# A gated convolution and its output projection become one stage, the projection's rows of two chunks first; the MLPs' down products wait for the half of the hidden rows that each panel uses

## The reference, cut to what matters

```python
def mixer_b(h, w_in, conv_w, w_out):
    b_gate, c_gate, xt = jnp.split(h @ w_in, 3, axis=-1)
    u = c_gate * xt
    y = lax.conv_general_dilated(u, ...)          # depthwise, three taps along the tokens
    return (b_gate * y) @ w_out

def mlp_sq_relu(h, w1, w2):
    return jnp.square(jax.nn.relu(h @ w1)) @ w2   # 1024 -> 4096 -> 1024

for i in range(DEPTH_2):
    y = rms_norm_2(h, norm1[i])
    y = mixer_a(...) or mixer_b(...)              # layer 0: attention, layer 1: mixer_b
    h = h + y
    h = h + mlp_sq_relu(rms_norm_2(h, norm2[i]), mlp_w1[i], mlp_w2[i])
```

## Time and profile before

| what | before |
|---|---|
| median of three runs | 3050.26 us |
| the profiled execution's own time | 3053.55 us |
| its span | 3051.8 us |
| PE busy | 2784.8 us, 91% |
| DVE, ACT, POOL busy | 37%, 30%, 26% |

### The profile page before, as it was taken

How to read it: one execution, slowest core, us unless ns; L and a number is a source line. 1 busy time by engine, 2 the same in 40 slices (tenths; PEclk the granted TensorE clock), 3 DMA queues, 4 the chain that set the end, 5 groups by cost and what they waited for, 6 DMA issues and landing times. The chain is left out here.

```text
span 3051.8 us, 56007 instructions
## 1 busy us (share of the span) xinstructions
PE 2784.8 (91%) x25293; PEld 2147.4 (70%) x25293; DVE 1119.5 (37%) x1536; ACT 921.8 (30%) x1462; POOL 789.0 (26%) x222
## 2 busy tenths in 40 slices
PE   6987988888896988989999999988999999899998
PEld 4765877777774423333689989987888778678887
DVE  3424765666346000101454556363211123321111
ACT  3123322432432100010444555553322222132222
POOL 3220431231210000000232332321444434334443
PEclk8998999999997999999999999999999999999999
DMA  7111201013041999999322221321223323223321
GB/s 260 56 32 39 70 17 61 4 60 102 4 133 42 420 427 426 427 427 426 135 79 73 80 70 56 84 83 56 91 97 98 99 72 97 83 83 97 97 97 56
DMA packets 171635, 397.69 MB, mean 130 GB/s; under 512 B 9552, under 2 KB 99637, under 8 KB 146037
## 3 DMA queue, kind: packets, MB, share of 16 engines
q1 hardware_dynamic: 170416, 390.70, 34.9%
q10 hardware_dynamic: 980, 3.40, 0.3%
HBM read 387.71 MB, written 4.19 MB: 128 GB/s over the span
## 5 line engine op out<-in xcount | busy, mean ns | idle before, releaser
L179 POOL TENSOR_TENSOR weight_ring_lo<-weight_ring,weight_hi 128x2048 fp32r<-128x2048 f32 (+1 forms) x144 | 656.5, 4559 | 1928.0 <-ACT weight_hi L168 1887.6
L168 ACT CAST weight_hi<-weight_ring 128x2048 fp32r<-128x2048 f32 (+1 forms) x144 | 271.2, 1885 | 640.3 <-PE late L226 339.7
L226 PE MATMUL late<-weight_hi,latT_hi 128*128 128x512 f32 x572 | 175.3, 429 | 0.0
L207 PE MATMUL late<-latT_hi,weight_hi 128*128 128x512 f32 x680 | 167.9, 389 | 0.0
L207 PE MATMUL late<-latT_lo,weight_hi 128*128 128x512 f32 x680 | 167.9, 389 | 0.0
L207 PE MATMUL late<-latT_hi,weight_ring_lo 128*128 128x512 f32 x680 | 167.9, 389 | 0.0
L1924 POOL TENSOR_TENSOR rws_E<-rws_AT,rw_tri 128x768 f32<-128x768 f32 x40 | 83.5, 2112 | 284.4 <-DVE rws_AT L1808 183.7
L226 PE MATMUL late<-weight_ring_lo,latT_hi 128*128 128x512 f32 x572 | 156.5, 396 | 0.0
L226 PE MATMUL late<-weight_hi,latT_lo 128*128 128x512 f32 x572 | 155.8, 394 | 0.0
L226 PE MATMUL late<-weight_hi,mlp_hid_hi 128*128 128x512 f32 x512 | 138.7, 393 | 9.8 <-issue 9.8
L3278 DVE TENSOR_TENSOR x<-x,late 128x512 f32<-128x512 f32 x64 | 44.0, 687 | 280.8 <-PE late L226 280.8
(11 more groups left out here) (630 smaller groups left out, 5339.5 us busy)
## 6 DMA issues: line engine op xcount, KB each, us to landing
weight_ring<-in_mlp_w SPq DMA_DIRECT2D x64, 1024.0 KB, 5.2
weight_ring<-in_a_wqkv SPq DMA_DIRECT2D x36, 1024.0 KB, 4.8
weight_ring<-in_w_up SPq DMA_DIRECT2D x32, 1024.0 KB, 20.2
weight_ring<-in_w_gate SPq DMA_DIRECT2D x31, 1024.0 KB, 22.2
weight_ring<-in_w_down SPq DMA_DIRECT2D x31, 1024.0 KB, 21.0
weight_ring<-in_w_mod SPq DMA_DIRECT2D x24, 1024.0 KB, 5.5
weight_hi_spare<-in_w_up SPq DMA_DIRECT2D x12, 1024.0 KB, 19.9
weight_hi_spare<-in_w_gate SPq DMA_DIRECT2D x12, 1024.0 KB, 22.2
```

The costliest lines, as they stand in the source:

```text
L168: self.nc.scalar.copy(self.view(self.hi[:, q % 2], p, True), self.view(self.slots[self.slot[p]], p, True)).then_inc(self.hi_ready, 1)
L179: self.nc.gpsimd.tensor_tensor(self.view(self.lo[:, s], p, True), self.view(self.slots[s], p, True), self.view(self.hi[:, q % 2], p, True) ...
L207: last = nc.tensor.matmul(dst, left(a, k), right(b, k), start=(a + b + k == 0), stop=(a == 1 and k == KD - 1))
L226: last = nc.tensor.matmul(dst, left(a, HK * r + k), right(b, k), start=(r + a + b + k == 0), stop=(r == 1 and a == 1 and k == HK - 1))
```

## The change

`gated_conv` takes over the projection: the four panels of `b_wout` are multiplied in the same block, behind the last chunk's panels, and its calls to the norm come with it. The panels are now ordered rows first, as those of `w_out` already are: first rows 0 to 511 (the first two chunks of z) for both halves of the columns, then rows 512 to 1023. PE waits for the copies of b and c (banks 0 to 3 are free), for two z chunks before the first two panels (`lowered`), for all four before the last two, and within the second panel it does the tiles of banks 6 and 7 first and waits for `emptied` ahead of banks 4 and 5. In `mlp` the one wait ahead of a quarter's down panels becomes two: the first down panel waits for two hidden chunks, the second for four.

```diff
@@ -3202,8 +3202,8 @@
                         else:
                             last = dense(nc, up[i % 2][h][:], left, right)
                 else:
-                    if n == 0:
-                        pe.wait_ge(hidden, NP * (q + 1))
+                    if n < 2:
+                        pe.wait_ge(hidden, NP * q + NP // 2 * (n + 1))
                     for j in range(NT):
                         u = NT * (2 * q + n // 2) + j
                         if n % 2 == 0 and u >= NT:
@@ -3289,7 +3289,7 @@
     return norm
 
 
-def gated_conv(nc, g, yT, z_hi, z_lo, banks, ahead):
+def gated_conv(nc, g, yT, z_hi, z_lo, banks, ahead, x, norm_of):
 
     sem, st = g.sem, g.stream
     p0 = st.taken
@@ -3297,17 +3297,22 @@
     copied = sem("gc_b_c_copied")
     rounded = sem("gc_rounded")
     step = Tally(sem("gc_steps"))
-    n_chunk = D // PW
+    lowered = sem("gc_lowered")
+    filled = sem("b_wout_filled")
+    added = sem("b_wout_first_half_added")
+    n_chunk, n_panel = D // PW, 2 * D // WIDE
+    p1 = p0 + 3 * n_chunk
     with ExitStack() as tmp, nc.Block() as block:
         bc = tmp.enter_context(nc.sbuf_tensor("gc_bc", [P, 2, 2, 2, T], F32))
         u = tmp.enter_context(nc.sbuf_tensor("gc_u", [P, 2, T], F32))
         y = tmp.enter_context(nc.sbuf_tensor("gc_y", [P, 2, T], F32))
         z = tmp.enter_context(nc.sbuf_tensor("gc_z", [P, 2, 2, T], F32))
         acc = [banks[2 * s:2 * s + 2] for s in range(3)]
+        norm = norm_of(tmp, [b[:] for b in banks])
 
         @block.sync
         def _(sp):
-            st.load_until(sp, p0 + 3 * n_chunk)
+            st.load_until(sp, p1 + n_panel)
 
         @block.tensor
         def _(pe):
@@ -3326,10 +3331,27 @@
                     else:
                         last = dense(nc, acc[part][h][:], left, right)
                 last.then_inc(st.used, 1)
+            for n in range(n_panel):
+                w = st.take_split(pe)
+                c, r = n % 2, n // 2
+                if n == 0:
+                    pe.wait_ge(copied, 2 * n_chunk)
+                if c == 0:
+                    pe.wait_ge(lowered, n_chunk // 2 * (r + 1))
+                for j in (2, 3, 0, 1) if n == 1 else range(NT):
+                    if n == 1 and j == 0:
+                        pe.wait_ge(emptied, n_chunk)
+                    last = dense_half(nc, banks[NT * c + j][:], lambda a, k: (z_hi, z_lo)[a][:, k, j * P:(j + 1) * P],
+                                      lambda b, k: w[b][:, k, :], r)
+                    if r and j + 1 < NT:
+                        last.then_inc(filled, 1)
+                last.then_inc(st.used, 1)
+            pe.wait_ge(added, 1)
+            norm.turn(pe)
 
         @block.gpsimd
         def _(pool):
-            st.reduce_until(pool, p0 + 3 * n_chunk + 2)
+            st.reduce_until(pool, p1 + n_panel + 1)
 
         @block.scalar
         def _(act):
@@ -3353,6 +3375,14 @@
                     split(c - 1)
                 st.round_until(act, p0 + 3 * c + 5)
             split(n_chunk - 1)
+            st.round_until(act, p1 + n_panel + 1)
+            for j in range(NT):
+                norm.square(act, j)
+                if j:
+                    norm.root(act, j - 1)
+            norm.root(act, NT - 1)
+            for k in range(LEAD):
+                norm.round(act, k)
 
         @block.vector
         def _(dve):
@@ -3363,7 +3393,7 @@
 
             def lower(c):
                 dve.wait_ge(rounded, c + 1)
-                V.tensor_tensor(z_lo[:, 2 * c:2 * c + 2], z[:, c % 2], z_hi[:, 2 * c:2 * c + 2].bitcast(F32), ALU.subtract)
+                V.tensor_tensor(z_lo[:, 2 * c:2 * c + 2], z[:, c % 2], z_hi[:, 2 * c:2 * c + 2].bitcast(F32), ALU.subtract).then_inc(lowered, 1)
 
             for c in range(n_chunk):
                 if c:
@@ -3389,6 +3419,24 @@
                 last.then_inc(emptied, 1)
                 dve.wait_ge(emptied, c + 1)
             lower(n_chunk - 1)
+            for c in range(2):
+                for j in range(NT):
+                    if j + 1 < NT:
+                        dve.wait_ge(filled, (NT - 1) * c + j + 1)
+                    else:
+                        dve.wait_ge(st.used, p1 + 3 + c)
+                    d = x[:, j, c * WIDE:(c + 1) * WIDE]
+                    last = V.tensor_tensor(d, d, banks[NT * c + j][:], ALU.add)
+                    if c:
+                        last.then_inc(norm.x_ready, 1)
+                        if j:
+                            norm.scale(dve, j - 1)
+                if c == 0:
+                    last.then_inc(added, 1)
+            norm.scale(dve, NT - 1)
+            for k in range(LEAD):
+                norm.lower(dve, k)
+    return norm
 
 
 def program(nc, a, out):
@@ -3450,9 +3498,12 @@
             st.add((w[:, r0 + hp * P:r0 + (hp + 1) * P], 0), (w[:, r0 + 512 + hp * P:r0 + 512 + (hp + 1) * P], P), n_slot=3)
         st.add_matrix(a["w_mod"], 0, 2 * D, 6 * D - D // 2, split=False, n_slot=2)
         st.add_matrix(a["w_mod"], 0, 6 * D - D // 2, 6 * D, split=False)
-        for r in range(0, D, D // 2):
-            for c in range(0, D, WIDE):
-                st.add((a["w_out"][r:r + D // 2, c:c + WIDE], 0), row=WIDE)
+        def add_rows_first(w):
+            for r in range(0, D, D // 2):
+                for c in range(0, D, WIDE):
+                    st.add((w[r:r + D // 2, c:c + WIDE], 0), row=WIDE)
+
+        add_rows_first(a["w_out"])
         st.add_slots([None] * 4, [lasting(f"slot{s}_full") for s in range(SLOTS, SLOTS + 4)])
 
         def add_gate_up(e):
@@ -3488,7 +3539,7 @@
         for c in range(0, D, PW):
             for part in range(3):
                 st.add((a["b_win"][:, part * D + c:part * D + c + PW], 0))
-        st.add_wide(a["b_wout"], 0, 0, D)
+        add_rows_first(a["b_wout"])
         add_mlp(1)
 
         with ExitStack() as first:
@@ -3683,8 +3734,7 @@
             with ExitStack() as tmp:
                 z_hi = g.sb_in(tmp, "gc_z_hi", [P, KD, T], F32R)
                 z_lo = g.sb_in(tmp, "gc_z_lo", [P, KD, T], F32R)
-                gated_conv(nc, g, yT, z_hi, z_lo, banks, ahead)
-                ahead = project_rows(nc, g, "b_wout", lambda i, k: (z_hi, z_lo)[i][:, k], x, normed("norm2_1", "norm2", 1, True), banks)
+                ahead = gated_conv(nc, g, yT, z_hi, z_lo, banks, ahead, x, normed("norm2_1", "norm2", 1, True))
             mlp(nc, g, "mlp1", yT, x, banks, ahead, store=(output_stored, by_token(out)))
 
 
```

## The result

The changed kernel takes 3023.29 us (median of four runs, 3020.65 to 3024.74), the one before 3050.94 beside it (3049.55 to 3052.37). The ratio is 0.9909, with a 95% interval of 0.9894 to 0.9925; of 3050.9 us that is a gain of 23 to 32 us, 27.65 by the medians. Forecast were 3022.6 us and 27.6. Of all executions behind the ratios in this document one was slow, 4430.39 us for the rows-first kernel in two blocks, and its ratio leaves it out.

The account below looks back on a forecast made before the run. PE's work plus its holes was taken to set the time: 24.15 us of holes, 1.89 and 1.57 us of slow matmuls make 27.6 us, so 3050.26 falls to 3022.6 us. The range was 3018.5 to 3027.5 us.

Parts of the forecast that it names:

- The holes and their sizes: PE's idle holes would go: 14.07 us ahead of the convolution's projection, 5.04 us in each MLP, 24.15 us together.
- What would be late next: Nothing late: margins 2.7 us (third b_wout panel), about 0.7 us (MLPs' down panels); late residuals, 3027.5 us, chance 0.07.
- The barrier and the order: Ahead of the projection, the last chunk's data, not the block's end, were said to cause the 14.07 us hole.
- The second panel's tile order: In the second b_wout panel, banks 6 and 7 go first, lasting to 2642.29; `emptied` is there 4.9 us early.
- The slow matmuls behind the holes: First twelve matmuls behind each hole run slow: 1.89 us at the projection, 1.44 and 1.70 in the MLPs, 5.03 together.
- half of the 3.14 us: Behind the MLPs' two short holes, only 1.57 us of slow matmuls were counted as gain against the median.
- It gave 0.19 to none of it being paid: Rival: slow matmuls behind the holes were the profiled execution's own; only 24.15 us go, 3026.1 us, chance 0.19.
- The sum against the profiled execution (29.2 us): All holes and slow matmuls, 24.15 plus 5.03 us, would take the profiled 3053.55 us to 3024.4.
- The rival with a chance of 0.07: Tail behind the convolution's projection: the norm's transposes fall into the slow clock, 2.4 us lost, 3025.0 us, chance 0.07.
- The longer stretches: Rival: MLP stretches 43.5 us longer without a hole make the chip halve the clock, 3110 us, chance 0.02.

Follow-up runs that it names:

- the rows-first kernel in two blocks: The kernel before with b_wout's panels ordered rows first, the projection still a block of its own: 3051.34 against 3051.77 us, ratio 0.9999.
- The added pass: The changed kernel with one more POOL pass into a scratch tile between the second and third b_wout panels' residuals: 3030.12 us, one execution.
- the stage alone: The changed kernel with the old single wait back in `mlp`, so only the convolution's stage is changed: 3035.19 us, ratio 0.9939 to the kernel before.
- the MLPs' wait alone: The kernel before with only the wait ahead of each quarter's down panels split in two: 3039.27 against 3051.77 us, ratio 0.9958.
- the columns first: The changed kernel, blocks joined, with b_wout's panels ordered by columns again: 3021.47 us, ratio 0.9916 to the kernel before.
- With the hole filled: The changed kernel with eight unread matmuls ahead of the third tile's transposes in three norms: 3017.49 us, ratio 0.9897 to the kernel before.
- early roots: The changed kernel with ACT taking each tile's root right behind its squares, in three norms: 3012.07 us, ratio 0.9882; again 3013.45 us, 0.9883.

## Why the prediction was right

- **The holes and their sizes.** Right. 24.15 us of holes were named, and PE's waits show them gone, in each part's run those of its own edit. The segments shrank by 6.7, 15.9 and 6.5 us where hole plus slow matmuls were 6.74, 15.96 and 6.48.
- **What would be late next.** Right: nothing. The tightest margins came out at 2.6 and 0.7 us. The added pass shows that the 2.6 us are real: a chain 3.3 us late made a wait of 0.6.
- **The barrier and the order.** The lengths were right (13.8 us of chain on the last chunk, 10.9 us of cover by a panel), but the prediction is wrong where it says that the data and not the end of the block caused the hole. In the old order too the first panel needs rows 0 to 511 alone, whose z_lo was there before 2623.06, 17 us ahead of PE's start. It was the block's end that held PE back, until DVE had finished a chunk that this panel doesn't use: with the blocks joined and the old order kept, PE runs the first panel at once, and only 3.05 us of hole are left for the data. The two halves alone give 0 (order without the joined stage) and 11.1 of 16.0 us (joined stage without the order), so both are needed.
- **The second panel's tile order.** Taken as a detail; it is worth 0.9 us.
- **The slow matmuls behind the holes.** Mis-sized, by the term "half of the 3.14 us". The prediction took only half of the 3.14 us behind the MLPs' holes, as a thing that might differ between executions, because the profiled one was 3.3 us above the median; the part ahead of the attention's tail, which varies by more than that, can explain such a difference as well. It gave 0.19 to none of it being paid. In the three kernels that keep these holes unfilled (before, the stage alone, rows first in two blocks) the six MLP segments are 354.97 to 355.21 us, and 348.3 to 348.5 in all that have no hole: 6.5 to 6.9 us, each time. The sum against the profiled execution (29.2 us) was the true one for these segments.
- **The norm's tail.** The rival with a chance of 0.07 came true beside the forecast. The tail behind the projection was 7.58 us in the three kernels with the hole of 13.9 us (before, the MLPs' wait alone, rows first in two blocks), and 8.6 to 9.2 us in the seven profiles where that hole was gone or filled and the tail itself unchanged. It was priced at up to 2.4 us, by taking 24 transposes at full clock for 2.9 us where 3.26 can be reached; it costs 1.0 to 1.6. Why the clock stays up in the tail when it had dropped some 45 us earlier is open, and it isn't a rule of that kind: with the columns first it had dropped 38 us ahead of the tail, which was slow all the same (8.61). The hole of 2.29 us doesn't decide it alone. Of the twenty tails behind the first MLP and the projection that have it, ten had slow transposes (8.4 to 9.2 us) and ten had none (7.6). With the hole filled none was slow, in one profile.
- So the mechanism was right, and the agreement to 0.1 us is luck: two errors cancel, 1.57 us too little for the slow matmuls and 1.57 us for a tail that was taken to stay as it was. The interval of 23 to 32 us couldn't have told them anyway.
- **The longer stretches.** That the longer unbroken stretches would cost the clock is refuted: PEclk is 1.00 in all of them, and the second MLP runs at its 0.2267 us a matmul to the end.

## What to carry to other kernels

When PE sets the time, list its waits, and for each work out which part of the data the next panel really uses: a wait for half of it lets one panel (10.9 us here) cover a chain of 5 us, and two panels one of 13.8 us. For a chain that ends in the stage before, it takes both an order of panels that starts with what is ready and no stage's end in between: the order alone gave 0 of 16 us, the joined stages alone 11. A wait that the profile puts down to a block's end, just when another engine's chain ends, has two possible causes, and what the next panel needs tells them apart. Then look at the short idle stretches that remain, since a hole of 2.3 us sometimes costs another 1.6 in slow transposes; taking the root one step earlier shortened these holes and brought 6.8 to 7.7 us over the three tails (27.7 and 28.6 us in the changed kernel's two profiles, 20.8 with early roots).

## What the runs showed of the hardware

- Half clock (1.2 GHz, PEclk 0.50) appeared behind PE's holes of 14, 5 and 3.05 us each time, behind 2.29 us in ten of the twenty tails named above, and not in the four tails behind the first MLP and the projection that had holes of only 0.8 and 1.0 us. Matmuls that nobody reads held it at 1.00 with all waits in place (12.86 us of them in the hole of 14, 4.69 in those of 5). With early roots the attention's tail still fell to half clock in both profiles (20 transposes in 4.07 us), and with 1.17 us of matmuls in the first of its holes it stayed up (2.40), in the one profile taken.
- The Trainium skill ("TensorE: Matmul & The Clock Gate", Part 1, "The HAM clock gate") says that the number of slow matmuls varies between runs. For the MLPs' holes the profiles don't bear that out (6.5 to 6.9 us in six places); for the tails they do (7.58 and 8.38 us for the same code behind the first MLP). Runs of transposes alone went through the clock's rise: in the second profile of the changed kernel the 24 behind the first MLP started at 0.50 (2479 to 2481 us) and ended at 1.00 (2482 to 2483).
- POOL's idle time isn't free for DVE: an added POOL pass of 4.04 us, whose result nobody waits for, delayed DVE's operations with two SBUF inputs by 3.3. "SBUF — State Buffer" ("SBUF: two separate sides") of the Trainium skill says that such an operation and a POOL operation that reads SBUF exclude each other for the whole instruction, and the trace agrees with it.
